# Two transformer blocks on one core: the second block's norms applied behind the products, with X transposed unscaled in halves

## What is computed

```python
for l in range(DEPTH):
    x = x + 0.5 * swiglu(rms_norm_2(x, ffn1_norm[l]), ffn1_wg[l], ffn1_wu[l], ffn1_wd[l])
    x = x + hybrid_mixer(rms_norm_2(x, mix_norm[l]), positions, rel_bias, w_in[l], ...)
    x = x + 0.5 * swiglu(rms_norm_2(x, ffn2_norm[l]), ffn2_wg[l], ffn2_wu[l], ffn2_wd[l])
return rms_norm_2(x, final_norm)

def swiglu(x, wg, wu, wd):
    return (jax.nn.silu(x @ wg) * (x @ wu)) @ wd
```

## Time and profile before

| | us |
|---|---|
| runs | 1722.57, 1727.37, 1728.58 |
| median | 1727.37 |
| span of the profiled execution, from its first to its last instruction | 1724.9 |
| busy in it: PE / PEld / DVE / ACT | 1482.1 / 853.4 / 740.2 / 454.2 |
| mean granted clock of PE | 0.955 |

### The profile page before, as it was taken

How to read it: one execution, slowest core, us unless ns; L and a number is a source line. 1 busy time by engine, 2 the same in 40 slices (tenths; PEclk the granted TensorE clock), 3 DMA queues, 4 the chain that set the end, 5 groups by cost and what they waited for, 6 DMA issues and landing times. The chain is left out here.

```text
span 1724.9 us, 26401 instructions
## 1 busy us (share of the span) xinstructions
PE 1482.1 (86%) x10287; PEld 853.4 (49%) x10287; DVE 740.2 (43%) x1420; ACT 454.2 (26%) x872; POOL 24.1 (1%) x48
## 2 busy tenths in 40 slices
PE   4999888887798999769977666759999999999998
PEld 3986622232232333213322111228888878888887
DVE  4736532423242232313322131337774546466764
ACT  2435310000010010000100000026553536265653
POOL 2002000000000000000000000000000000000000
PEclk9999999999899999899998888889999999999999
DMA  9849699999999999999999999972465731155460
GB/s 351 342 173 368 271 378 425 425 426 424 427 425 426 426 416 407 427 425 427 424 427 424 428 424 427 424 315 101 171 235 197 291 123 49 49 207 195 156 258 25
DMA packets 69014, 549.35 MB, mean 318 GB/s; under 512 B 6001, under 2 KB 6778, under 8 KB 44250
## 3 DMA queue, kind: packets, MB, share of 16 engines
q1 hardware_dynamic: 66392, 542.67, 76.6%
q0 software_dynamic: 1744, 3.53, 0.7%
q10 hardware_dynamic: 690, 0.48, 0.1%
HBM read 545.59 MB, written 1.07 MB: 317 GB/s over the span
## 5 line engine op out<-in xcount | busy, mean ns | idle before, releaser
L1326 PE MATMUL PS<-ring,arena 128*32 128x512 f32 x2768 | 345.3, 638 | 88.0 <-DMA ring<-in_w_gate_up 84.0
L1036 PE MATMUL PS<-ht_pair,weights_high 128*128 128x512 f32 x832 | 289.8, 392 | 3.0 <-DVE weights_low L1599 1.7
L1599 DVE TENSOR_TENSOR weights_low<-ring,weights_high 128x1024 fp32r<-128x1024 f32 x204 | 247.9, 1220 | 94.9 <-ACT weights_high L713 94.8
L1968 DVE TENSOR_SCALAR arena<-PS 128x256 f32<-128x256 f32 x47 | 19.9, 424 | 523.9 <-PE PS L1326 523.9
L1326 PEld LDWEIGHTS PS<-ring,arena 128*32 128x32 f32 x2768 | 86.0, 114 | 319.7 <-issue 185.7
L713 ACT ACTIVATE weights_high<-ring 128x1024 fp32r<-128x1024 f32 x204 | 214.3, 1057 | 88.8 <-PE PS L1032 88.7
L713 ACT ACTIVATE arena<-PS 128x256 f32<-128x256 f32 (+2 forms) x237 | 100.7, 432 | 514.9 <-PE PS L1383 345.2
L1038 PE MATMUL PS<-ht_pair,weights_low 128*128 128x256 f32 x832 | 232.8, 280 | 0.0
L1036 PEld LDWEIGHTS PS<-ht_pair,weights_high 128*128 128x128 f32 x832 | 155.7, 187 | 38.2 <-issue 4.0
L713 ACT ACTIVATE arena<-arena 128x256 f32<-128x256 f32 (+2 forms) x113 | 45.7, 405 | 452.0 <-DVE arena L1968 447.6
L1038 PEld LDWEIGHTS PS<-ht_pair,weights_low 128*128 128x128 f32 x832 | 157.2, 189 | 0.0
(11 more groups left out here) (275 smaller groups left out, 1587.0 us busy)
## 6 DMA issues: line engine op xcount, KB each, us to landing
ring<-in_w_gate_up SPq DMA_DIRECT2D x117, 2048.0 KB, 34.0
ring<-in_w_down SPq DMA_DIRECT2D x54, 2048.0 KB, 34.7
ring<-in_w_ada SPq DMA_DIRECT2D x6, 4096.0 KB, 17.0
ring<-in_w_in SPq DMA_DIRECT2D x6, 4096.0 KB, 13.0
arena<-in_w_gate_up SPq DMA_DIRECT2D x11, 2048.0 KB, 35.0
arena<-in_w_down SPq DMA_DIRECT2D x10, 2048.0 KB, 36.1
ring<-in_ffn_wg SPq DMA_DIRECT2D x4, 4096.0 KB, 13.9
ring<-in_ffn_wu SPq DMA_DIRECT2D x4, 4096.0 KB, 17.2
```

The lines of the kernel that those rows point to most:

```text
L1036: mm(PS[:, bank, :].rearrange("p (a t) -> p a t", a=2), high, HT_PAIR[:, :, k, :], start=first, stop=False, skip_group_check=True)
L1326: ins = mm(PS[CH * t:CH * (t + 1), c % INL, :].rearrange("p (u n) -> p u n", u=2), XTE[b][c % INL][:, KT // 2 * half + k, :], w[:, k % 2, ...
L1599: v.tensor_tensor(low, w, high, ALU.subtract).then_inc(sem("split_low"), 1)
```

## The change

- X itself is transposed, half by half (columns 0 to 511 and 512 to 1023 of 128 rows at a time): turn_half, into PSUM banks 2 to 5. Three of the four sets stand among the last sum products at norms 3 and 4, the fourth behind the first products on the new rows (fresh_unit, fresh_rows). The sums' last four pieces are ordered by half.
- The gain is still applied by ACT and DVE as they copy the turned columns (high_columns, low_columns), now without the token's scale. Mean and root come behind that.
- The scale comes behind the products. DVE puts each token's scale on a diagonal (SCALE_BY), PE multiplies it by ones so that every partition holds all 256 scales (spread_scale, behind the second unit), ACT copies that to SBUF (spread_out). Silu and sigmoid units are multiplied by it; transposed units of the mixer too (op "times", all on DVE now); token units take it by row. The mul units stay unscaled, and X's add behind the down projection takes the scale with its factor 0.5.
- DVE and ACT split two pieces within the norm, and the dummy products of norms 3 and 4 and behind the transposes are gone.
- The first slab of the first feed-forward block is loaded as two halves of its columns.

```diff
-KEEP_ROWS = {0: (0, 0), 1: (0, 16), 2: (5, 4), 3: (0, 5), 4: (0, 5)}
-KEEP_COLUMNS = {2: 2, 3: 8, 4: 4}
+KEEP_ROWS = {0: (0, 0), 1: (0, 16), 2: (5, 4)}
...
+        def scaled_units(slab, n0, dst, by):
+            for j in range(4):
+                unit("T", slab, n0 + j * P, "D", "times", dst[:, j, :], gate_tile=by)
+        def sum_pieces(slab, nk):
+            ks = list(range(0, nk, 2))
+            order = [(k, h) for k in ks[:-2] for h in range(2)] + [(k, h) for h in range(2) for k in ks[-2:]]
+            return [piece(slab, "tok", k, h * HALF) for k, h in order]
...
-        v_units(WIN2, 0, U2)
+        v_units(WIN2, 0, U2, "rows")
         mu = mark()
-        q_units(WIN2, HALF, QT2, "scale")
-        q_units(WIN2 + 1, 0, KT2, "copy")
-        v_units(WIN2 + 1, HALF, V2)
+        scaled_units(WIN2, HALF, QT2, SCALE_BY_8)
+        scaled_units(WIN2 + 1, 0, KT2, SCALE_BY)
+        v_units(WIN2 + 1, HALF, V2, "rows")
...
-                if g == WIN[0]:
-                    sp.dma_start(dst[:, :, 0:HALF], src[:, :, 0:HALF]).then_inc(sem("win_half"), 16)
+                if g in (WIN[0], FF1):
+                    sp.dma_start(dst[:, :, 0:HALF], src[:, :, 0:HALF]).then_inc(sem("win_half" if g == WIN[0] else "ffn_half"), 16)
                     dst, src = dst[:, :, HALF:D], src[:, :, HALF:D]
...
+                        if u["i"] in (m1[0], m3[0]):
+                            spread_out(2 if u["i"] == m1[0] else 4)
...
+            def spread_out(k):
+                act.wait_ge(sem("scale_mm"), k - 1)
+                if k == 3:
+                    f(SCALE_BY_8, PS[:, 6, 0:T], scale=DH ** -0.5)
+                f(SCALE_BY, PS[:, 6, 0:T]).then_inc(sem("scale_spread"), 1)
...
+            def high_columns(k, half, scale):
+                for kt in range(KT // 2 * half, KT // 2 * (half + 1)):
+                    bank, o = turned_at(kt)
+                    act.wait_ge(sem("norm_turned"), KT // 2 * k + kt // 2 + 1)
+                    f(HTH[:, kt, :], PS[:, bank, o:o + T], scale=scale[:, kt:kt + 1]).then_inc(sem("ht_high"), 1)
+            def columns_and_norm(k, scale):
+                half_squares(k, 0, 0)
+                half_squares(k, 0, 1)
+                split_until(split[0])
+                half_squares(k, 1, 0)
+                high_columns(k, 0, scale)
+                split_until(split[0])
+                half_squares(k, 1, 1)
+                high_columns(k, 1, scale)
+                norm_roots(k, 0)
+                norm_roots(k, 1)
+            def half_squares(k, tt, h):
+                act.wait_ge(sem("x_ver"), x_version(k, tt, h))
+                cols, o = slice(h * HALF, (h + 1) * HALF), tt if h == 0 else 80 + tt
+                ins = f(XN[:, tt, cols], X[:, tt, cols], ACT.Square, scale=D ** -0.5, accum_out=ST[:, o:o + 1])
+                if h:
+                    ins.then_inc(sem("norm_ssq"), 1)
...
+            def turn_half(k, tt, h):
+                pe.wait_ge(sem("x_ver"), x_version(k, tt, h))
+                for kt in range(KT // 2 * h, KT // 2 * (h + 1)):
+                    bank, o = turned_at(kt)
+                    ins = nc.tensor.transpose(PS[:, bank, o + tt * P:o + (tt + 1) * P], X[:, tt, kt * P:(kt + 1) * P], ident)
+                    if tt == 1 and kt % 2:
+                        ins.then_inc(sem("norm_turned"), 1)
+            def spread_scale(k):
+                pe.wait_ge(sem("scale_diagonal"), k - 1)
+                for tt in range(TT):
+                    ins = mm(PS[:, 6, tt * P:(tt + 1) * P], ones, SCALE_BY[:, tt * P:(tt + 1) * P], start=True, stop=True)
+                ins.then_inc(sem("scale_mm"), 1)
...
-                done_behind = {0: 1, 1: 2, 3: 1}
                 for tt in range(TT):
-                    for n in (0, 2, 1, 3):
-                        p, kt0, h = todo[-4:][n]
+                    for n, (p, kt0, h) in enumerate(todo[-4:]):
                         if tt == 0:
                             pe.wait_ge(sem("split_low"), p + 1)
                             if ready is not None:
                                 pe.wait_ge(sem(ready), kt0 + 2)
                         ins = tok_rows(p, tt, parts, kt0, 4 + 2 * tt + h, kt0 == 0, kt0 == last_kt)
-                        if tt == 1 and n in done_behind:
-                            ins.then_inc(sem("piece_mm"), done_behind[n])
-                        elif n >= 2:
+                        if tt == 1:
+                            ins.then_inc(sem("piece_mm"), 1)
+                        elif n % 2:
                             ins.then_inc(sem("first_rows_mm"), 1)
-            def unit_products(u0, u1, x, fresh=None):
+                        if norm is not None and (tt, n) in ((0, 3), (1, 1), (1, 2)):
+                            turn_half(norm, *{(0, 3): (0, 0), (1, 1): (0, 1), (1, 2): (1, 0)}[tt, n])
...
+            def fresh_unit(u0, norm):
+                u = units[u0]
+                bank_free(u)
+                p = u["pieces"][0]
+                pe.wait_ge(sem("split_low"), p + 1)
+                _, high, low = piece_views(p)
+                for k in range(KT):
+                    if k == KT // 2:
+                        turn_half(norm, 1, 1)
+                    pe.wait_ge(sem("ht_low"), KT * (norm - 2) + k + 1)
+                    ins = pair(u["i"] % 4, high[:, k, :], low[:, k, :], k, k == 0, k == KT - 1)
+                ins.then_inc(sem("piece_mm"), 1)
+            def fresh_rows(u0, norm):
+                for u in units[u0:u0 + 2]:
+                    bank_free(u)
+                for n, p in enumerate(units[u0]["pieces"]):
+                    pe.wait_ge(sem("ht_low"), KT * (norm - 2) + 2 * n + 2)
+                    tok_piece(p, (HTH, HTL), 2 * n, lambda tt: units[u0 + tt]["i"] % 4, n == 0, n == 3)
+                    if n == 0:
+                        turn_half(norm, 1, 1)
...
-            norm(2)
-            unit_products(m1[0], m2[0], (HTH, HTL), fresh=2)
+            for tt in range(TT):
+                keep_on(KEEP_ROWS[2][tt], 0)
+                for h in range(2 - tt):
+                    turn_half(2, tt, h)
+            fresh_unit(m1[0], 2)
+            unit_products(m1[0] + 1, m1[0] + 2, (HTH, HTL))
+            spread_scale(2)
+            unit_products(m1[0] + 2, m2[0], (HTH, HTL))
             down_products(0)
-            norm(3)
-            unit_products(m2[0], mv[0], (HTH, HTL), fresh=3)
+            fresh_rows(m2[0], 3)
+            spread_scale(3)
+            unit_products(mu[0], mv[0], (HTH, HTL))
...
-                            v.tensor_tensor(u["dst"], first, second, ALU.add).then_inc(sem("unit_D"), 1)
+                            link(v.tensor_tensor(second, first, second, ALU.add))
+                            dve.wait_ge(sem("scale_spread"), 1 if u["i"] < m2[0] else 2 if u["i"] < m3[0] else 3)
+                            v.tensor_tensor(u["dst"], second, SCALE_BY, ALU.mult).then_inc(sem("unit_D"), 1)
...
+            def low_columns(k, kt0, kt1, scale):
+                for kt in range(kt0, kt1):
+                    bank, o = turned_at(kt)
+                    dve.wait_ge(sem("ht_high"), KT * (k - 2) + (kt | 1) + 1)
+                    stt(HTL[:, kt, :], PS[:, bank, o:o + T], scale[:, kt:kt + 1], HTH[:, kt, :],
+                        ALU.mult, ALU.subtract).then_inc(sem("ht_low"), 1)
+            def columns_and_norm(k, scale, add):
+                split_until(split[0])
+                add(1, 0)
+                low_columns(k, 0, 2, scale)
+                add(1, 1)
+                low_columns(k, 2, 4, scale)
+                split_until(split[0])
+                row_mean(k, 0)
+                low_columns(k, 4, 7, scale)
+                row_mean(k, 1)
+                low_columns(k, 7, 8, scale)
                 for tt in range(TT):
-                    if add is not None:
-                        add(tt, 0)
-                        if tt:
-                            split_until(split[0])
-                        add(tt, 1)
+                    row_root(k, tt)
+                    v.tensor_scalar(ST[:, 82 + tt:83 + tt], ST[:, 6 + tt:7 + tt], 0.5, None, ALU.mult)
+                    ins = v.tensor_scalar(SCALE_BY[:, tt * P:(tt + 1) * P], ident, ST[:, 6 + tt:7 + tt], None, ALU.mult)
+                ins.then_inc(sem("scale_diagonal"), 1)
...
             post_mean(1, 0)
             post_gains(1, GGF, 1)
+            post_mean(1, 1)
             post_sum(1, 0)
-            post_mean(1, 1)
+            post_add(0, 0)
+            post_add(0, 1)
             post_sum(1, 1)
-            row_mean(2, 0)
-            row_root(2, 0)
-            scaled_rows(0)
-            row_mean(2, 1)
-            split_until(split[0])
-            row_root(2, 1)
-            scaled_rows(1)
-            norm_columns(2, VC[:, R_F1:R_F1 + 8], None)
+            columns_and_norm(2, VC[:, R_F1:R_F1 + 8], post_add)
```

146 lines of the change are left out of this document (74 added, 72 removed).

## The result

| | before | changed |
|---|---|---|
| median (lowest to highest) | 1727.37 us (1722.57 to 1728.58) | 1735.97 us (1734.26 to 1741.84) |
| ratio, 95% interval | | 1.0062 [1.0045, 1.0079] |
| profiled execution: span, mean clock | 1724.9 us, 0.955 | 1732.3 us, 0.956 |

A second measurement of the changed kernel, among the experiments, gave 1.0063 [1.0043, 1.0083]. 0.62% of 1725 is 10.7 us.

A forecast was written before the change was run, and what follows sets the result against it. PE was taken to set the pace in dense stages, with the change touching the norms between them. Terms 5.3 - 1.1 + 2.1 + 0.5 + 3.4 = +10.2 us, added to the 1727.4 median, gave 1737.6 us, range 1729 to 1743.

The forecast's parts named there:

- the chain of +12.75 from the copy: Norm 4: third unit starts 12.75 us after ACT's first copy; with the copy 3.2 us earlier, the net is +2.1 us.
- The step without a row of its own: Norm 4, spreading to third unit: PE spreads, ACT copies, DVE multiplies, then splits; 2.8 us, between 0.5 and 3.5.
- Norm 2, +5.3: Norm 2: first copy stays at 1165.9, third unit moves from 1173.3 to 1178.65, costing 5.3 us.
- Rival 2: Norm 2: PE returns earlier from the branch, copy 2.9 us earlier; +3.9 us in all, 1731.3 us; chance 0.10.
- the head start: Norms 3 and 4: ACT's first column copy comes about 3.2 us earlier, since transposes no longer wait for scaled rows.
- rival 4: Sum blocks: transposes between sum products wait for X and stretch the sums; 0 to +2 us more; chance 0.04.
- Norm 3: Norm 3: copy at 1350.8, third piece at 1360.7 instead of 1362.3, less 0.5 for spreading; -1.1 us.
- Gates, +0.5: Silu and sigmoid units: the added multiplications hide, except behind the attention, where they delay a late split; +0.5 us.
- The clock, +3.4: Norms 2 and 4: PE's 2.3 us waits behind the spreading each trigger a clock fall costing 1.7 us; +3.4 us.
- shorter ones: Norms 2 and 4: new PE waits of 0.7 and 1.5 us ahead of the waits behind the spreading.
- The halves of the slab, 0: First feed-forward slab at norm 2: loading in halves wins or loses nothing; 0 us, bounds 0 and -0.5.
- Rival 3: Norms 2, 3 and 4: early start counts in full, third unit within 8 us of copy; -7.3 us, 1720.1; chance 0.04.

The follow-up runs named there:

- split_first: Changed kernel, with DVE's split moved ahead of its wait for the spread scale at the first unit of norms 2 and 4; ratio 1.0034 to the kernel before.
- third_split: Changed kernel, with ACT and DVE splitting landed pieces ahead of the square roots in norms 2, 3 and 4; ratio 1.0016 to the kernel before.
- After_again: The changed kernel unaltered, measured and profiled once more; ratio 1.0063 to the kernel before.
- before_nobranch: Kernel before the change, without PE's program for crowded experts that it jumps over; ratio 0.9996 to the kernel before.
- before_nofill: Kernel before the change, without PE's filling products at norm 2; ratio 1.0008 to the kernel before.
- no_branch: Changed kernel, without PE's program for crowded experts that it jumps over; ratio 1.0042 to the kernel before.
- ts_nofill: third_split without PE's filling products at norm 2; ratio 1.0014 to the kernel before.
- keep: Changed kernel, with PE's short waits around the first unit of norms 2 and 4 filled by products with the unit matrix; ratio 1.0051 to the kernel before.
- one_load: Changed kernel, with the first dense slab loaded in one piece again; ratio 1.0060 to the kernel before.
- ts_both: third_split with both the edit of ts_turn and that of ts_nofill; ratio 0.9987 to the kernel before.
- ts_turn: third_split, with the last four transposes of norms 2 and 4 set two products earlier in the first unit; ratio 0.9998 to the kernel before.

## Why the prediction was right, and where it was not

The forecast was +10.2 us and 1737.6 us; the second block took 10.6 and 9.35 us more in two executions of the change, and the median is 1735.97. That the total came so close is in part luck: without the clock the terms add up to 6.8, and the two executions show about 7.4 and 7.9; for the clock 3.4 was put down, and they show 3.2 and 1.4.

- **Norm 4, the chain of +12.75 from the copy: right, 12.76.** The step without a row of its own (spreading to third unit, taken as 2.8 between 0.5 and 3.5) measured 1549.64 - 1546.81 = 2.83. Of the 5.2 us that the chain is longer than before (7.55), about half is lost in the first unit: from its first product to the second unit's it takes 5.66 us against 2.85, with the waits of 0.35 and 1.23 for columns and the last transposes in between (computed: second unit at +7.2, measured +7.15). The other half is the spreading and the wait of 2.23 behind it, and for that wait split_first and third_split show the reason given: the split behind the scale.
- **Norm 2, +5.3: right.** After_again has 12.90 from copy to third unit at a clock of 1.00, 5.4 more than before, and the copy 12.22 us behind D against 12.33. The reason was half right. The prediction said that PE's late return from the branch holds the copy in both kernels. Before, it was DVE's scaled halves (before_nobranch, before_nofill: no gain). In the change it was PE, by the jump and the filling products behind it: either taken away brings the copy to 9.85 us. Rival 2's 2.9 us measured 2.4. By the Trainium skill (Runtime: NRT & Kernel Launch, Instruction fetch mechanics) a jump past what is fetched makes the engine wait for its code; no_branch agrees, since the 7.2 us went with the branch. That earlier data wins nothing here does not follow from it: ts_nofill has the jump and the early copy, since X was there by then but for its last half (a wait of 0.44 us), and in the change only the filling products stood between.
- **Norms 3 and 4, the head start: right, and a little too large.** The terms of this stretch are -3.2 (norm 4's copy), -1.1 and +0.5, -3.8 in all; t2 to c4 shows -3.2 and, in after_again, -2.7. At norm 4 itself, from DVE's first add to X to the copy, it is 1536.88 - 1528.68 = 8.20 us against 11.29 before: 3.1 less. PE's waits at norms 3 and 4 have none for X (its weight loads waited once, 0.30 us), so rival 4 did not occur beyond that. Norm 3 behaved as laid out; the timeline of the change against the earlier trace rows:

```profile
1356.31 1.55 ACT L729 ACTIVATE ht_pair<-PS,veccols 128x256 fp32r<-128x256 f32 x4
...
1366.33 0.47 PE L1072 MATMUL PS<-weights_high,ht_pair 128*128 128x512 f32 x1 [1.84 <-DVE weights_low L1685]
```

  Copy to third piece 10.0 us, where 1360.7 - 1350.8 = 9.9 was computed.
- **Gates, +0.5: right, 0.4.** The wait behind the attention, 1.14 us in the earlier trace rows, is 1.52; the 60 multiplications took 25.5 us of DVE, hidden elsewhere:

```profile
1446.74 0.47 PE L1078 MATMUL PS<-ht_pair,weights_high 128*128 128x512 f32 x1 [1.52 <-DVE weights_low L1685]
```

```profile
L1710 DVE TENSOR_TENSOR arena<-arena 128x256 f32<-128x256 f32 x60 | 25.5, 425 | 7.2 <-ACT arena L729 5.3
```

- **The clock, +3.4 by two falls of 1.7 behind the spreading: about the size, wrong in the place.** The changed kernel lost 2.3 us in the first unit of norm 2 and 0.9 in PE's opening; after_again 1.4 at norm 4. In both, the falls came at waits that the prediction had named as "shorter ones" ahead and given no price. Two executions of the same code with the fall at different norms show that the earlier trace rows could not give a place. Five kernels keep the idle stretches of 2.23 us, ten stretches in all: six passed at 1.00 (both in each execution of the change, one each in keep and one_load), and behind four the clock fell within 1.5 us (keep at norm 2, one_load at norm 4, no_branch at both). When a stretch of this length is followed by a fall stays open.
- **The halves of the slab, 0: right** (one_load).
- **Rival 3**, the head start in full, needed a third unit within 8 us of the copy. ts_both comes to 9.67 and, with the copy 2.5 us earlier at norm 2, ends level with the kernel before or just below it; the 7.3 us that the rival would win are far off.

## What to carry to other kernels

When a step is moved so that another can begin sooner, ask what stands behind the new wait in each engine's order: here an early start of 3 us was lost to a chain 5.2 us longer. Two splits stood behind a multiplication that needed the moved result, and a line that let the splits go first recovered nearly half of the kernel's loss. An engine idle ahead of a stage can be held by the work placed there to bridge the idle time; it was free before, when other data came later, and on the path once that data came sooner. Judge such changes by distances between events within a trace: here the spans also held some 6 us of variation from the stages before.

## What was not expected

- **The last stage has two paces at full clock.** t4 to end is 182.5 to 182.7 us in seven executions and 184.9 in three (keep, split_first, ts_both); the 184.3 of one_load and no_branch hold a fall of the clock (1.7 us) behind t4. Behind the stage's first product there is no wait, and the clock reads 1.00 up to the last units in both; the same 336 products are busy 116.6 us in one and 118.8 in the other. By form, PE from norm 4's third unit on, third_split and then keep (whose 2.2 us of waiting is ahead of the first product):

```profile
L1079 PE MATMUL PS<-ht_pair,weights_high 128*128 128x512 f32 x336 | 116.6, 394 | 0.0
```

```profile
L1079 PE MATMUL PS<-ht_pair,weights_high 128*128 128x512 f32 x336 | 118.8, 399 | 2.2 <-DVE weights_low L1691 2.2
```

  Before_nofill and before_nobranch show the slow one too (399 ns), and one_load and before_nofill have it in the stage behind norm 2 as well, so it goes with the stage and the execution, not with these edits alone. The cause is open, and none was tried. It puts 2.2 us on ts_both's profiled execution.
- **Filling products do not decide the clock alone.** Without them PE stayed at half clock in ts_nofill from the transposes of norm 2 on for 13 us, through the whole first unit, and ran that unit at full clock in ts_both. Single looks at a clock cannot rank such edits; the times can, and there ts_both against ts_turn (0.9987 and 0.9998, with intervals that overlap) leaves the worth of leaving them out unsettled.
